# Attention: the softmax factors move from a GpSimd multiplication of the probabilities into a diagonal operand of the turning product

## The reference, cut to what matters

```python
for blk in range(S // Q_BLOCK):
    q0, q1 = blk * Q_BLOCK, (blk + 1) * Q_BLOCK
    s = (jnp.einsum('bqhd,bkhd->bhqk', q_nope[:, q0:q1], k_nope[:, :q1])
         + jnp.einsum('bqhd,bkd->bhqk', q_rope[:, q0:q1], k_rope[:, :q1])).astype(jnp.float32) * scale
    mask = frame_chunk[None, :q1] <= frame_chunk[q0:q1, None]
    prob = jax.nn.softmax(jnp.where(mask, s, -jnp.inf), axis=-1).astype(v.dtype)
    outs.append(jnp.einsum('bhqk,bkhd->bqhd', prob, v[:, :q1]))
```

## Time and profile before

| | us |
|---|---|
| median of 3 runs | 3408.01 (3407.78 to 3411.37) |
| the profiled execution, its own time | 3409.32 |
| its span | 3407.8 |
| PE busy in the span | 3071.8 |
| POOL busy in the span | 1084.1 |
| attention's steady part, from 1105 us to 1525 us | 420 |

### The profile page before, as it was taken

How to read it: one execution, slowest core, us unless ns; L and a number is a source line. 1 busy time by engine, 2 the same in 40 slices (tenths; PEclk the granted TensorE clock), 3 DMA queues, 4 the chain that set the end, 5 groups by cost and what they waited for, 6 DMA issues and landing times. The chain is left out here.

```text
span 3407.8 us, 45604 instructions
## 1 busy us (share of the span) xinstructions
PE 3071.8 (90%) x15074; PEld 2545.3 (75%) x15074; DVE 1649.9 (48%) x2730; ACT 1066.7 (31%) x2363; POOL 1084.1 (32%) x1228
## 2 busy tenths in 40 slices
PE   7999997868886797979969999989998999999898
PEld 5888884657775676867857888868886788887686
DVE  3653005446664564546666555675554533333333
ACT  2111014334443554542233333433332311111321
POOL 2322241165651766630035333363332000000122
PEclk9999998889998998999989999999999999999899
DMA  3211216412223211015543222222222533332543
GB/s 138 82 74 74 74 61 187 158 51 78 72 61 87 60 44 56 29 42 191 173 156 136 74 87 79 74 74 85 81 80 79 194 94 99 95 102 89 169 125 101
DMA packets 284043, 329.32 MB, mean 97 GB/s; under 512 B 32897, under 2 KB 224257, under 8 KB 279553
## 3 DMA queue, kind: packets, MB, share of 16 engines
q1 hardware_dynamic: 238248, 265.84, 24.7%
q0 software_dynamic: 12384, 45.09, 3.8%
q10 hardware_dynamic: 33280, 16.78, 1.7%
HBM read 210.73 MB, written 116.92 MB: 96 GB/s over the span
## 5 line engine op out<-in xcount | busy, mean ns | idle before, releaser
L1987 PE MATMUL ff_bank<-ff_x_hi,ff_w_lo 128*128 128x512 f32 x1240 | 487.4, 393 | 39.9 <-DVE ff_w_lo L2167 18.3
L1988 PE MATMUL ff_bank<-ff_x_lo,ff_w_hi 128*128 128x512 f32 x1240 | 486.2, 392 | 0.0
L1989 PE MATMUL ff_bank<-ff_x_hi,ff_w_hi 128*128 128x512 f32 x1240 | 485.6, 392 | 0.0
L1970 POOL TENSOR_TENSOR ff_w_sum<-ff_w_raw 128x512 f32<-128x512 f32 x210 | 293.2, 1406 | 507.5 <-DVE ff_w_lo L2167 446.6
L1987 PEld LDWEIGHTS ff_bank<-ff_x_hi,ff_w_lo 128*128 128x128 f32 x1240 | 235.1, 190 | 91.5 <-DVE ff_w_lo L2167 27.3
L222 PE MATMUL in_h_ps<-in_x_hi,in_w_lo 128*128 128x512 f32 x704 | 277.4, 394 | 25.4 <-POOL in_w_lo L178 25.4
L2369 PE MATMUL fd_acc<-fd_w_hi,fd_a_lo 128*128 128x512 f32 x704 | 277.1, 394 | 21.2 <-DVE fd_a_lo L2353 21.1
L223 PE MATMUL in_h_ps<-in_x_lo,in_w_hi 128*128 128x512 f32 x704 | 276.6, 393 | 0.0
L224 PE MATMUL in_h_ps<-in_x_hi,in_w_hi 128*128 128x512 f32 x704 | 276.4, 393 | 0.0
L2370 PE MATMUL fd_acc<-fd_w_lo,fd_a_hi 128*128 128x512 f32 x704 | 275.0, 391 | 0.0
L2371 PE MATMUL fd_acc<-fd_w_hi,fd_a_hi 128*128 128x512 f32 x704 | 275.0, 391 | 0.0
(11 more groups left out here) (371 smaller groups left out, 6603.7 us busy)
## 6 DMA issues: line engine op xcount, KB each, us to landing
ff_w_raw<-w_gate_up SPq DMA_DIRECT2D x44, 1024.0 KB, 5.2
scratch_hT<-in_out SPq DMA_DIRECT2D x22, 1024.0 KB, 3.9
fd_a_raw<-scratch_hid SPq DMA_DIRECT2D x176, 128.0 KB, 2.1
dr_qkv<-scratch_hT SPq DMA_DIRECT2D x16, 768.0 KB, 5.1
in_w_raw<-w_in POOLq DMA_DIRECT2D x22, 512.0 KB, 3.9
scratch_hid<-ff_first SPq DMA_DIRECT2D x44, 256.0 KB, 2.3
scratch_hid<-ff_second SPq DMA_DIRECT2D x44, 256.0 KB, 2.3
in_x_raw<-xT SPq DMA_DIRECT2D x8, 1024.0 KB, 4.9
```

The costliest lines, as they stand in the source:

```text
L1970: pool.tensor_tensor(w_sum[:, SUM_SLOT[m]], w_raw[:, b, one], w_raw[:, b, two], op).then_inc(w_sum_done, 1)
L1987: pe.matmul(acc, w_lo[:, wm, ws], x_hi[:, xm, k], start=first_mm, stop=False, skip_group_check=skip)
L1988: pe.matmul(acc, w_hi[:, wm, ws], x_lo[:, xm, k], start=False, stop=False, skip_group_check=skip)
L1989: return pe.matmul(acc, w_hi[:, wm, ws], x_hi[:, xm, k], start=False, stop=last_mm, skip_group_check=skip)
```

## The change

A new tile `diag` holds, for each of the two buffers, two query tiles and up to four groups, a 128 by 128 matrix. POOL no longer touches `prob`. For each block it makes one multiplication of the identity, repeated over tiles and groups, by `scale`, repeated along each row: the result is the diagonal matrix of the factors. It raises `scaled` as before. `turn` uses a plain product of the probabilities (stationary) with that diagonal matrix (moving) where it used PE's transpose operation with the identity; all operands are float32. The number of turned tiles, their places and the order around them stay.

```diff
+        diag = s.sb("diag", [P, 2, 2, 4, P])
...
+            pool.wait_ge(const_sem, 4)
...
                     pool.wait_ge(scale_done, N * i + n + 1)
                     pb, g = n % 2, groups[n]
-                    ops = []
-                    for tile in range(2):
-                        if g > 1:
-                            view = prob[:, pb, tile, 0:NTOK * (g - 1)].rearrange("p (g n) -> p g n", n=NTOK)
-                            ops.append((view, scale[:, pb, tile, 0:g - 1].unsqueeze(2).broadcast_to([P, g - 1, NTOK])))
-                        w = widths(j, tile)[-1]
-                        view = prob[:, pb, tile, NTOK * (g - 1):NTOK * (g - 1) + w]
-                        ops.append((view, scale[:, pb, tile, g - 1:g].broadcast_to([P, w])))
-                    for view, by in ops:
-                        op = pool.tensor_tensor(view, view, by, ALU.mult)
-                    op.then_inc(scaled, 1)
-                    if pieces(2 * i + b, n):
-                        pool.wait_ge(scaled, N * i + n + 1)
+                    shape = [P, 2, g, P]
+                    pool.tensor_tensor(diag[:, pb, :, 0:g], ident[:].unsqueeze(1).unsqueeze(1).broadcast_to(shape),
+                                       scale[:, pb, :, 0:g].unsqueeze(3).broadcast_to(shape), ALU.mult).then_inc(scaled, 1)
...
-                        last = pe.transpose(pT_ps[:, k % T_RING, at:at + P], src, ident[:])
+                        by = diag[:, n % 2, tile, p // 2]
+                        last = pe.matmul(pT_ps[:, k % T_RING, at:at + P], src, by, start=True, stop=True)
```

## The result

The changed kernel takes 3416.64 us, the kernel before 3408.74 us (medians of 20 runs each, in turns). The ratio is 1.0021, with a 95% interval from 1.0012 to 1.0031: some 7 to 8 us slower, where 20 were forecast. One execution of the changed kernel took 8071 us; the median of the other 19 is 3416.17 us. Of the attention stage, from the start of its first score product to that of its last value product, the traces show 424.6 us after (1105.3 to 1529.9) and 417.8 before (1103.7 to 1521.5): +6.8 us. It leaves out what varies from one execution to the next elsewhere: in the traces of the fourteen kernels, which all have the same code there, the part ahead of the stage took 1098.9 to 1112.1 us and the part behind it 1884.5 to 1891.5.

A forecast was written before the change was run, and what follows sets the result against it. PE was taken to set the attention stage's pace, with about 60 us of idle time to absorb added work. 61.7 - 8.6 - 32.4 - 1.5 + 1.0 = +20.2 us gave 3428 us, range for 8 in 10 3414 to 3456.

The forecast's parts named there:

- The turning product: PE's turn: a plain float32 product runs as two passes, 0.1135 us more a tile, +61.7 us over 544 tiles.
- POOL's part, -8.6: PE's 11 waits for POOL's multiplication shrink or go, since making diagonals is shorter: -8.6 us.
- the clock, -1.5: PE's slow clock after the 3.17 us idle stretch near 1301 us should go: -1.5 us.
- short waits and heads: PE's waits for POOL: heads and last blocks of rounds shrink by 1.4 us, five short waits vanish, 2.8 us.
- the late block of round 1: Block at 1301.11 us where POOL came late and PE waited 3.17 us: 2.7 us of that wait saved.
- that of round 2: Corresponding block of the second round: PE's wait of 1.67 us for POOL gone, multiplication falling from 2.96 to 1.04 us.
- The idle time taken up, -32.4: PE's waits for low parts absorb added work: 28.8 us in four-to-eight-pair blocks, 3.6 in two- and three-pair blocks.
- the 1.0 us for tiles turned at the slow clock: Some ten tiles at the head of the rounds, turned at 1.2 GHz, where the second pass costs twice: +1 us.
- all idle time but the head's is taken up: Rival, 12%: all PE idle time but the head's absorbed and the clock recovers, +6 to +10, about 3416 us.
- Waits that move along whole: Rival, 13%: low parts shift with the slower turn, nothing but POOL's part is taken up, +53, 3461 us.
- One pass in this place: Rival, 6%: the turning product runs as one pass, pace staying at 0.11 us; -9, 3399 us.
- Four times the transpose: Rival, 4%: the plain turning product costs four times the transpose; +127, 3535 us.

The follow-up runs named there:

- the one with one pass: Changed kernel with probabilities and diagonals stored as float32r, rounded to that type, one record a tile: stage 407.1 us; 3398.97 us, ratio 0.9961.
- the kernel with the diagonals alone: Changed kernel, but the turn is the transpose with the identity, softmax factors left out of the result: stage 406.6 us; 3398.85 us, ratio 0.9969.
- the product alone: Kernel before, its transpose replaced by a plain float32 product with the identity, POOL still multiplying: stage 436.1 us, +18.3; 3430.54 us, ratio 1.0067.
- the two halves: The product alone against the kernel before (stage +18.3 us, 3430.54 us) and the kernel with the diagonals alone (stage -11.2 us, 3398.85 us).
- The experiment on one wait: Kernel before, 9 and 14 added value products ahead of values 1 in one seven-pair and one eight-pair block a round: 3411.13 us, ratio 1.0003.

## Why the prediction was off

**The turning product.** Right: 1088 records, two passes, 0.1125 to 0.1135 us more a tile. The run with two transposes a tile and the one with one pass close it from both sides.

**POOL's part, -8.6, and the clock, -1.5.** Right in sum, -11.2 measured, and wrong in what makes it. Forecast: short waits and heads 4.2, the late block of round 1 and its clock 4.2, 1.67 for that of round 2. Measured: 3.79 and 0.99 for the two late blocks, nothing to speak of for the short waits and heads, 0.6 for the clock in the block of two pairs behind the border, and 6.1 in blocks with DVE's long small operations, which the prediction did not see (shown for 4.4 of it). That the sum is near is luck. The short waits went where it had not looked: in the first block of three pairs PE's wait of 0.72 us for POOL and of 1.31 for `pT_lo` became, in the kernel with the diagonals alone, two for `pT_lo`, 0.46 and 1.55, and the block stayed at 10.20 us. PE was held there by what came behind the turn, the low parts, and the multiplication was not the last link. The late block is as forecast; the changed kernel near 1300 us and across the border, in the columns of the earlier trace rows:

```profile
1300.00:1304.00 4.00, 3.56 (x27) 3.27 (x27) 2.08 (x9) 1.22 (x4) 1.99 (x3) 1.00 0.30 78
1316.00:1332.00 16.00, 9.99 (x38) 8.64 (x39) 2.89 (x9) 3.06 (x9) 0.61 (x1) 0.56 0.06 20
```

PE's granted clock is 1.00 where it was 0.66, with the idle stretch of 3.17 us gone, and still 0.56 at the border, where PE idles as before.

**The idle time taken up, -32.4.** This is the step that failed, and by its size alone. The prediction named the right waits and had them vanish, and they did: 40.2 us to 9.5. But it took the length in the list for what a wait can take up. Measured with the product alone, it was 43.4 us: 11 us more, which is nearly the whole error of the forecast. The rest: POOL's part and the clock gave 1.1 more than forecast, and the 1.0 us for tiles turned at the slow clock is in the 18.3 already: 20.2 - 11.0 - 1.1 - 1.0 = 7.1, the sum of the two halves; measured 6.8. Per wait: the block of seven pairs with waits of 0.34 and 0.89 us took up 27 x 0.1135 - 1.22 = 1.84 us, 0.30 more for each; the one of eight pairs, 31 x 0.1135 - 1.74 = 1.78; that of six pairs in round 2, with 0.90 and 0.41, 23 x 0.1135 - 0.77 = 1.84, 0.27 more for each. Over some 42 waits that vanished, 0.27 each is 11 us. The experiment on one wait shows the same from the other side, 0.89 listed and 1.1 taken up, and its rows show the cause for the greatest part: the bracket starts at the modelled end of a record, up to 0.28 us (a turning group 0.60) behind its start, while PE starts the next in 0.115. Read by starts, the 38 waits behind a turn last 0.245 us longer than listed, and the product behind them 0.02 more, which is the 0.27. So the mechanism is in the rows of the whole stage; by added work it was tried on the one kind of wait alone.

One number of the text ahead was wrong besides: the block of the earlier trace rows has eight pairs and 31 tiles, not seven and 27. The seven-pair block ahead of it has the same two waits, so the reckoning (+1.8, measured +1.22) fits that one; for the block itself it would have been +2.3, measured +1.74.

**The rivals.** The one that came nearest was that all idle time but the head's is taken up, +6 to +10: near in time, but not what happened, since 9.5 us of waits stay and the clock at the border did not recover (0.56). It comes near because the waits that did vanish took up more than the list has. Waits that move along whole are there only at the end of a round (1.17 us before and after); in blocks of two to four pairs 0.15 to 0.99 us of each is left. One pass in this place was not so; made so on purpose, it gave 3399 us, the time that the rival named, though a good part of that gain came over DVE. Four times the transpose was not so. In the two profiled executions the part ahead of the stage is 1.6 us longer and the part behind it 2.4, less than they differ among kernels with the same code there.

## What to carry to other kernels

To learn what idle time can take up, measure it from start to start against the same pair of instructions where nothing waits; a list of waits that counts from an instruction's modelled end gives less by a fixed amount for each wait (0.16 or 0.245 us here), which weighs most where the waits are short. Before moving work between engines, look at the small instructions of a third engine: if a few numbers take several times what they take elsewhere, compare when they end with when the busy engine's instruction ends. A change that helps in one size of block and harms in another is worth splitting by size.

## What was not expected of the hardware

A DVE operation over two small SBUF tensors took 0.16 us by itself and 0.58 us beside a POOL instruction, ending with it; the mean of the eight instructions of one size went from 156 up to 439 ns, while a reduction of the same size kept 156 to 162 ns in the kernels compared. A float32 product of 128 by 128 cost what two transposes do (436.1 against 434.7 us of stage, 0.2225 against 2 x 0.109 us from start to start), and a float32r one what one does (407.1 against 406.6).
